# Column sums of modulation blocks in a diffusion-transformer step on one core: TensorE products with ones, or TensorE transposes summed by ScalarE

## The chip, the core and the metric

The kernel runs on one core of one Trainium2 chip. Its engines are TensorE (PE for its matmuls, PEld for its weight loads), VectorE (DVE), ScalarE (ACT), GpSimd (POOL) and SyncE (SP, which issues nearly all DMAs). Each engine works through its own instructions in the order in which they were written and waits on semaphores that the others raise. The metric is the device time of one execution in microseconds. The median of the runs is quoted.

## What is computed

One layer of an inference step for 1024 latent tokens and 256 context tokens, width 1024, in float32. What matters here is the modulation. From the conditioning vectors `c` (latent) and `c_ctx` (context) it makes six vectors of 1024 for each of the two token groups, and these shift, scale and gate the layer's two halves:

```python
def _modulation(cond, w_mod, b_mod):
    m = jax.nn.silu(cond) @ w_mod + b_mod
    return jnp.split(m[:, None, :], N_MOD, axis=-1)
...
    shift1, scale1, gate1, shift2, scale2, gate2 = mod
    h = _rmsnorm(x, norm1_g) * (1 + scale1) + shift1
    u = h @ w_in
    ...
    x = x + gate1 * (merged @ w_out)
    h2 = _rmsnorm(x, norm2_g) * (1 + scale2) + shift2
    a, b = jnp.split(h2 @ w_gu, 2, axis=-1)
    x = x + gate2 * ((jax.nn.silu(a) * b) @ w_down)
```

`u` feeds three mixers: neighbourhood attention, a pooling mixer and a convolution module. A final RMSNorm follows.

## The kernel before

**Number format of the matmuls.** A large product is done in three matmuls (`products`, L152): weights and activations are split into an upper part rounded to a shorter format and the rest (hi, lo, AH, AL). ACT makes the upper parts and DVE or POOL the lower ones.

**Three stages** follow each other: the front (`front_engines`: norm, input projection, pooling and convolution mixers; up to about 332 us), attention with the gate projections beside it (`attention_engines`), and the rear (`rear_engines`: output projections, second norm, and the FFN from about 1080 us on).

**The front.** The input projection has 18 units of 128 output channels, each in three token chunks `(u, c)` of 512, 512 and 256 columns. PE runs 24 matmuls a chunk and writes them to banks 0 to 3 of PSUM in a ring. A bank is given back by ACT, or, for units 1 and 3 and the channel mean, by DVE (`after`, `freed`). Banks 4 and 5 serve transposes of keys and values.

**Modulation.** The first two vectors (shift1, scale1) are made by PE at the start. The other four are made with little work for PE: DVE multiplies a block of `w_mod` by the conditioning values, one value for each row, and adds up eight such row groups (`modulation(n)` of the vector engine, L822 and L825), which leaves 128 partial sums in the partitions for each output channel. What is left to do is to sum over the partitions, so that the result has channels in the partitions. PE does this by a matmul with the accumulator as weights and a column of ones as the moving operand.
- *Late blocks* (gate1, shift2, scale2): n = 0 to 11, each of 256 channels for two token groups, thus four products of 128x128 with 128x1 (L441). Their results go to 48 columns of bank 7 (`modp`). `MOD_AT` (L115) says after which chunk PE does block n: n = 0 after (2, 2), 1 and 2 after (3, 0) and (3, 1), 3 and 4 after (4, 0) and (4, 1), 5 after (5, 0), 6 after (13, 2), 7 after (14, 0), 8 and 9 after (15, 0) and (15, 1), 10 after (16, 1), 11 after (17, 0). `mod_acc` has two buffers, so DVE waits in block n for PE's block n-2. At the end of the front ACT copies the 48 columns out at once (L805), and DVE adds the bias (`late_mod`).
- *The second gate* (gate2): n = 0 to 7, each of 128 channels, thus two products (L2411), with one accumulator `gate2_acc`. Their results go to 16 columns of bank 7 (`MOD_BANK`). ACT copies them out at p = 8 (L2825), and DVE adds the bias at p = 9 (`gate2_bias`).

**The FFN's order.** It goes over pairs p of hidden tiles with a seven-product scheme (P1 to P7, and X0, X1 for the context tokens). PE's order is `PRODUCTS`: for pair p it ends with P1 of pair p+1, then P4 and P3 of p, and right after P3 comes `gate2_products(p)`. The products go through a ring of banks 0 to 6. ACT's iteration p copies weights of pair p+1 to their upper parts (`upper_slot`, L2654, eight in all), copies P1 of p+1 (`copy_product`), and, when p is even, does the Silu of five quarters (`gate_quarter`, L2677). The last of them, "12", stands at the iteration's end and needs `add(p, "12")` of DVE (L3033), which needs P3 of p. POOL makes the lower parts of the slots (L2881), and DVE the weight sums in between.

**Other lines that are named:** L143 and L261 (`freed`, `after`), the evacuations L633 to L645 and L794 (the pool products), L833 (DVE's GLU product of unit 1 or 3, whose end frees banks), L452 (channel mean), L477 and L485 (transposes of keys and values), L1360 and L1367 on (attention on ACT).

Of the kernel before, what the change touches and what calls it, by code (L numbers as in the profile page):

```python
# [16 lines left out]
ACT = mybir.ActivationFunctionType  # L17
# [3 lines left out]
P = 128  # L21
D = 1024
KD = D // P
# [146 lines left out]
def front_engines(g, W, held):  # L170

    nc = g.nc
    with ExitStack() as ctx:
# [71 lines left out]
        STEPS = 2 * KD  # L245
        modp = g.aux[:, 1, 0:2 * 3 * KD]
        banks = g.ps_all[:, 0:2, :]
# [160 lines left out]
        def tensor(pe):  # L408
# [26 lines left out]
            def modulation(n):  # L435

                pe.wait_ge(acc_step, STEPS * (n + 1))
                for m in range(2):
                    for j in range(2):
                        c = 4 * n + 2 * m + j  # L440
                        mm = nc.tensor.matmul(modp[:, c:c + 1], mod_acc[:, n % 2, j, m * P:(m + 1) * P],  # L441
                                              g.ones[:, 0:1], start=True, stop=True)
                mm.then_inc(mod_used, 1)
# [171 lines left out]
        def scalar(act):  # L615
# [31 lines left out]
            def token_major(u, parts):  # L647
# [8 lines left out]
                for part in parts:  # L656
# [4 lines left out]
                    nc.scalar.activation(vt[:, a:b, :], flip[:, (at + part) % 2, 0:(b - a) * P].rearrange("p (t n) -> p t n", n=P), ACT.Copy).then_inc(tok_ready, 1)  # L661

            def cached_k_out():
                act.wait_ge(ck_turned, 1)
                for h in range(2):
                    nc.scalar.activation(cached_kT[:, 2 * h:2 * h + 2, :], flip[:, h, :].rearrange("p (a t) -> p a t", a=2), ACT.Copy).then_inc(ck_out, 1)
# [95 lines left out]
            for u in range(MIX):  # L762
# [6 lines left out]
                for c in range(3):  # L769
                    if u not in (0, 1, 3):  # L770
                        evacuate(u, c)
                    if c != 1 and U_V < u <= U_Q:
                        token_major(u - 1, (0, 1) if c == 0 else (2,))
                if u and u + 2 <= MIX and u != U_POOL:
                    split(u + 2)
# [21 lines left out]
                if u == 15:  # L797
                    for t in range(2):
                        act.wait_ge(ln_step, 1 + 2 * (t + 1))
                        for n, at in ((LAT, 0), (CTX, CCTX)):  # L800
                            x = conv[:, t, at:at + n]
                            nc.scalar.activation(x, x, ACT.Silu, bias=g.cols[:, OFF["cn_b"] + t:OFF["cn_b"] + t + 1],
                                                 scale=g.cols[:, OFF["cn_g"] + t:OFF["cn_g"] + t + 1]).then_inc(silu_ready, 1)
            act.wait_ge(mod_used, NG)
            nc.scalar.activation(g.mod[:, 2 * KD:5 * KD, :], modp.rearrange("p (m j) -> p m j", j=2), ACT.Copy).then_inc(mod_out, 1)  # L805

        def vector(dve):
# [78 lines left out]
            def late_mod():  # L886
                dve.wait_ge(mod_out, 1)
                mod = g.mod[:, 2 * KD:5 * KD, :]
                nc.vector.tensor_tensor(mod, mod, g.cols[:, OFF["b_mod"] + 2 * KD:OFF["b_mod"] + 5 * KD].rearrange("p (m j) -> p m j", j=1).broadcast_to([P, 3 * KD, 2]),
                                        ALU.add).then_inc(mod_step, 1)  # L890
                dve.wait_ge(mod_step, 1)
                mod_gain(g, 1, "norm2_g", 4, mod_step)
# [847 lines left out]
def rear_engines(g, G, sem, attention):  # L1740
# [3 lines left out]
    with ExitStack() as ctx:  # L1744
# [24 lines left out]
        gate2_acc = at("gate2_acc", [P, 2, P], N0 + 16384)  # L1769
        w_gate2 = W.raw[:, :].rearrange("p (k n) -> p k n", n=P)  # L1770
        hidden_in = at("hidden_in", [P, KD, T], -20480 - ROW)
        raw_rows = at("w_down_rows", [P, KD, T], -20480 - 2 * ROW)
# [523 lines left out]
        def tensor(pe):  # L2296
# [109 lines left out]
            def gate2_products(n):  # L2406
                if n == 0:
                    pe.wait_ge(*released(last_ring_job(MOD_BANK)))
                pe.wait_ge(acc_step, STEPS * (n + 1))
                for j in range(2):  # L2410
                    mm = nc.tensor.matmul(g.ps_all[:, MOD_BANK, 2 * n + j:2 * n + j + 1], gate2_acc[:, j, :], g.ones[:, 0:1], start=True, stop=True)  # L2411
                mm.then_inc(gate2_done, 1)

            def down_bank_wait(name, m):
                if name in ("P1", "P2"):
                    n = 4 * ROUND[name] + m
                    if n == MOD_BANK:
                        pe.wait_ge(gate2_out, 1)
                    else:
                        pe.wait_ge(*product_read(*[product for i, product in enumerate(RINGED) if i % PRODUCT_RING == n][-1]))  # L2420
                elif name != "ctx":
                    pe.wait_ge(*emptied(DOWN_PRODUCTS[ROUND[name] - 2], m))
                elif m % 2 == 0:
                    pe.wait_ge(*emptied("P5", m // 2))
# [116 lines left out]
        def scalar(act):  # L2541
# [114 lines left out]
            def copy_product(p):  # L2656
# [8 lines left out]
                nc.scalar.activation(temp[TEMP["11"][side]][:, :], g.ps_all[:, product_bank(p, "P1"), :], ACT.Copy).then_inc(copied, 1)  # L2665

            def gate_quarter(i, name):
                p = 2 * i
# [129 lines left out]
            for p in range(PAIRS_FFN):  # L2798
# [22 lines left out]
                if side == 0:  # L2821
                    gate_quarter(i, "12")
                if p == KD:
                    act.wait_ge(gate2_done, KD)
                    nc.scalar.activation(g.mod[:, 5 * KD:6 * KD, :], g.ps_all[:, MOD_BANK, 0:2 * KD].rearrange("p (m j) -> p m j", j=2), ACT.Copy).then_inc(gate2_out, 1)  # L2825
            for n in range(len(DOWN)):
# [84 lines left out]
        def vector(dve):  # L2911
# [149 lines left out]
            def gate2_bias():  # L3061
                dve.wait_ge(gate2_out, 1)
                gate2_mod = g.mod[:, 5 * KD:6 * KD, :]
# [414 lines left out]
```

## Time and profile before

| what | value |
|---|---|
| median of 3 runs | 1873.34 us (1871.3 to 1873.45) |
| profiled execution | 1871.09 us, span 1869.3 us |
| PE busy | 1847.3 us, 99% |
| DVE busy | 1145.8 us, 61% |
| ACT busy | 758.2 us, 41% |
| POOL busy | 543.7 us, 29% |
| granted clock of PE | 0.998 of full speed |

The span is the time from the first to the last record of the profiled execution. A timeline row gives the start, the length, the engine, the line, what it writes and reads, its form and how many like it were merged. The time in square brackets is how long the engine stood idle before it, with the instruction that released it. Ends of matmuls are modelled, and a matmul of 512 columns reads 0.39 us while the next begins 0.23 us after it. So the cost of something to PE is read from starts, not from lengths. A float32 product with ones shows as two matmul records, a transpose as one. Times of ACT and DVE are lengths of single instructions, which overlap a little at their ends.

### The profile page before, as it was taken

How to read it: one execution, taken by the hardware profiler on the slowest of the kernel's cores; microseconds unless marked ns; L12 is line 12 of the kernel's file. 1: busy time of each engine (PE TensorE's matmuls, PEld its weight loads, DVE VectorE, ACT ScalarE, POOL GpSimd, SP SyncE). 2: the span in 40 equal slices, each digit the busy share in tenths (PEclk: the TensorE clock that was granted, in tenths of full speed). 3: DMA queues.
4: the chain of work that ended last, by engine and by line, in shares of the span. 5: the costliest groups of instructions: out<-in, count | busy, mean ns of one | idle time of the engine just before them, and what ended most of it. 6: DMA issues, size and time to landing. Idle time of an engine off the chain costs nothing.

```text
span 1869.3 us, 27109 instructions
## 1 busy us (share of the span) xinstructions
PE 1847.3 (99%) x10106; PEld 1587.0 (85%) x10106; DVE 1145.8 (61%) x2142; ACT 758.2 (41%) x1444; POOL 543.7 (29%) x407
## 2 busy tenths in 40 slices
PE   8999999999999999999999999999999999999998
PEld 3788888888888888888888888888888888888898
DVE  4799996156566655366317855554434434789984
ACT  5612232355555564454313522222222222545464
POOL 0000000455555552144532144444344441000000
PEclk9999999999999999999999999999999999999999
DMA  8472545464444532756532222221222224866665
GB/s 325 161 221 62 148 128 192 120 151 115 112 119 112 126 95 75 239 169 185 180 116 68 82 77 96 96 84 58 74 74 74 74 74 150 283 209 224 210 212 204
DMA packets 243466, 260.52 MB, mean 139 GB/s; under 512 B 50696, under 2 KB 182280, under 8 KB 242312
## 3 DMA queue, kind: packets, MB, share of 16 engines
q1 hardware_dynamic: 243336, 258.80, 44.8%
q8 instruction: 81, 1.33, 0.3%
q14 instruction: 49, 0.40, 0.1%
HBM read 196.09 MB, written 62.65 MB: 138 GB/s over the span
## 4 chain that ended last, share of the span: by engine, by line
PE 90%; DVE 4%; DMA 2%; ACT 2%; issue 1%; POOL 0%; SPq 0%; ACTq 0%; DVEq 0%; POOLq 0%
PE ps_all L152 68%; PE ps_all L2452 5%; PE ps_all L2454 4%; PE ps_all L2453 4%; PE ps_all L1315 2%; PE ps_all L1301 2%; DVE mod_acc L825 1%; PE ps_all L1287 1%; DMA wmod_then_mixers<-w_mod_dram 1%; PE ps_all L1292 1%; PE ps_all L537 1%; DMA wmod_block<-w_mod_dram 1%; DVE Y L3114 0%; POOL KB L1520 0%; PE ps_all L2486 0%
## 5 line engine op out<-in xcount | busy, mean ns | idle before, releaser
L152 PE MATMUL ps_all<-AH,w_hi 128*128 128x512 f32 (+1 forms) x1376 | 493.7, 359 | 2.4 <-ACT gate_rows L1360 1.3
L152 PE MATMUL ps_all<-AH,w_lo 128*128 128x512 f32 (+1 forms) x1376 | 483.1, 351 | 0.0
L152 PE MATMUL ps_all<-AL,w_hi 128*128 128x512 f32 (+1 forms) x1376 | 483.0, 351 | 0.0
L152 PEld LDWEIGHTS ps_all<-AH,w_lo 128*128 128x128 f32 x1376 | 259.9, 189 | 36.0
L152 PEld LDWEIGHTS ps_all<-AH,w_hi 128*128 128x128 f32 x1376 | 260.2, 189 | 34.3 <-DVE AL L909 2.0
L152 PEld LDWEIGHTS ps_all<-AL,w_hi 128*128 128x128 f32 x1376 | 260.5, 189 | 30.1
L3033 DVE TENSOR_TENSOR quarter<-ps_all,quarter 128x512 f32<-128x512 f32 x140 | 96.6, 690 | 176.6 <-PE ps_all L152 174.6
L2881 POOL TENSOR_TENSOR slot_lo<-w_pair,slot_hi 128x512 fp32r<-128x512 f32 x96 | 129.9, 1378 | 174.0 <-ACT slot_hi L2654 174.0
L152 PE MATMUL ps_all<-AH,slot_hi 128*128 128x256 f32 (+1 forms) x384 | 129.5, 337 | 0.0
L152 PE MATMUL ps_all<-AL,slot_hi 128*128 128x256 f32 (+1 forms) x384 | 129.2, 336 | 0.0
L152 PE MATMUL ps_all<-AH,slot_lo 128*128 128x256 f32 (+1 forms) x384 | 129.1, 336 | 0.0
L2881 POOL TENSOR_TENSOR w_lo<-w_pair,w_hi 128x512 fp32r<-128x512 f32 x64 | 85.4, 1356 | 114.4 <-ACT w_hi L2654 114.4
L1469 DVE TENSOR_TENSOR PT<-ps_all,PT 128x384 fp32r<-128x384 f32 (+1 forms) x144 | 63.7, 479 | 79.7 <-ACT PT L1378 79.6
L1538 POOL TENSOR_SCALAR prob<-prob,softmax_cols 128x640 f32<-128x640 f32 (+1 forms) x80 | 60.5, 756 | 130.5 <-DVE softmax_cols L1462 125.4
L1367 ACT ACTIVATE prob<-ps_all,softmax_cols 128x256 f32<-128x256 f32 x80 | 38.0, 474 | 137.4 <-DVE softmax_cols L1452 123.9
L845 DVE SCALAR_TENSOR_TENSOR xT_then_mixers<-wmod_then_mixers,cols,xT_then_mixers 128x1295 f32<-128x1295 f32 x60 | 89.4, 1573 | 0.0
L2452 PE MATMUL ps_all<-AH 128*128 128x512 f32 (+1 forms) x248 | 86.9, 350 | 1.1 <-DVE AL L3069 1.1
L1514 POOL TENSOR_TENSOR w_lo<-w_raw,w_hi 128x1024 fp32r<-128x1024 f32 x21 | 50.5, 2404 | 124.6 <-ACT w_hi L1338 124.6
L2454 PE MATMUL ps_all<-AH,AL 128*128 128x512 f32 (+1 forms) x248 | 86.3, 348 | 0.0
L2453 PE MATMUL ps_all<-AL,AH 128*128 128x512 f32 (+1 forms) x248 | 86.3, 348 | 0.0
L2452 PE MATMUL ps_all<-AH,w_hi 128*128 128x512 f32 (+1 forms) x236 | 83.9, 355 | 0.0
L2454 PE MATMUL ps_all<-AH,w_lo 128*128 128x512 f32 (+1 forms) x236 | 83.3, 353 | 0.0
(309 smaller groups left out, 4084.6 us busy)
## 6 DMA issues: line engine op xcount, KB each, us to landing
w_raw<-w_in_dram SPq DMA_DIRECT2D x42, 512.0 KB
w_pair<-w_gu_dram SPq DMA_DIRECT2D x20, 1024.0 KB, 5.3
hidden_in<-hidden SPq DMA_DIRECT2D x77, 256.0 KB, 3.5
wmod_then_mixers<-w_mod_dram SPq DMA_DIRECT2D x19, 1024.0 KB, 8.0
hidden<-quarter SPq DMA_DIRECT2D x50, 256.0 KB, 2.1
branch_and_gates<-gates SPq DMA_DIRECT2D x16, 768.0 KB, 4.4
w_down_rows<-w_down_dram SPq DMA_DIRECT2D x44, 256.0 KB, 3.7
gates<-gate_rows SPq DMA_DIRECT2D x42, 256.0 KB, 2.5
```

What stands on the lines that cost most here:

```text
L152: mm = nc.tensor.matmul(out, w, a[:, k, cols[0]:cols[1]], start=(first and part == 0), stop=(last and part == 2))
L845: nc.vector.scalar_tensor_tensor(conv[:, t, :], glu[:, t, k:k + CV], w, conv[:, t, :], ALU.mult, ALU.add).then_inc(conv_step, 1)
L1301: mm = nc.tensor.transpose(psT[:, turned_at(j):turned_at(j) + P], prob[:, s % 3, j * P:(j + 1) * P], g.ident[:, :])
L1367: nc.scalar.activation(pr[:, LOCAL:PCOLS], psS_past, ACT.Exp, bias=c[:, 2:3], accum_out=c[:, 4:5]).then_inc(past_ready, 1)
L1469: nc.vector.tensor_tensor(PT[:, s % 2, j0:j1, P:2 * P], psT[:, turned_at(j0):turned_at(j0) + (j1 - j0) * P].rearrange("p (j n) -> p j n", ...
L1514: nc.gpsimd.tensor_tensor(W.lo[:, u % 2, :], W.raw[:, :], W.hi[:, u % 2, :].bitcast(F32), ALU.subtract).then_inc(W.lo_ready, 1)
L1538: nc.gpsimd.tensor_scalar(pr[:, a:PCOLS], pr[:, a:PCOLS], c[:, 5:6], 1.0, ALU.mult, ALU.mult).then_inc(normal, 1)
L2452: nc.tensor.matmul(out, wh, th, start=first, stop=False)
L2453: nc.tensor.matmul(out, wh, tl, start=False, stop=False)
L2454: return nc.tensor.matmul(out, wl, th, start=False, stop=last)
L2881: nc.gpsimd.tensor_tensor(tiles4(lo), in_pair(p, idx), tiles4(hi.bitcast(F32)), ALU.subtract).then_inc(s_lo, 1)
L3033: nc.vector.tensor_tensor(temp[TEMP[out][side]][:, :], g.ps_all[:, product_bank(p, source), :], temp[TEMP[first][side]][:, :], ALU.add).th ...
```

## The change

PE no longer multiplies the accumulator blocks by ones. It turns each 128x128 block by a transpose, which puts channels in partitions and the partial sums along the free axis. ACT then copies each turned block onto itself in PSUM, and its accumulator output, the sum along the free axis, goes straight to the block's column of `g.mod`.

In the front the turned blocks of n go to the whole of bank 6 or bank 7 in turn. PE waits before block n for ACT's sums of block n-2, and ACT does `mod_sums(n)`, four copies, right after the chunk's evacuation and the token-major copies. The copy of 48 columns is gone, and DVE's `late_mod` waits for all 12 sums.

For the second gate both turned blocks of n go to the same 256 columns of bank 7 each time. PE waits in group n for ACT's sums of group n-1, and ACT does `gate2_sums(p-1)`, two copies, at the end of its iteration p, for p = 1 to 8. The copy of 16 columns is gone.

```diff
@@ -243,7 +243,7 @@
         STEPS = 2 * KD
-        modp = g.aux[:, 1, 0:2 * 3 * KD]
+        mod_turns = g.aux
         banks = g.ps_all[:, 0:2, :]
@@ -435,11 +435,12 @@
                 pe.wait_ge(acc_step, STEPS * (n + 1))
+                if n >= 2:
+                    pe.wait_ge(mod_out, n - 1)
                 for m in range(2):
                     for j in range(2):
-                        c = 4 * n + 2 * m + j
-                        mm = nc.tensor.matmul(modp[:, c:c + 1], mod_acc[:, n % 2, j, m * P:(m + 1) * P],
-                                              g.ones[:, 0:1], start=True, stop=True)
+                        at = (2 * m + j) * P
+                        mm = nc.tensor.transpose(mod_turns[:, n % 2, at:at + P], mod_acc[:, n % 2, j, m * P:(m + 1) * P], g.ident[:, :])
                 mm.then_inc(mod_used, 1)
@@ -660,6 +661,15 @@
+            def mod_sums(n):
+                act.wait_ge(mod_used, n + 1)
+                for m in range(2):
+                    for j in range(2):
+                        at, row = (2 * m + j) * P, 2 * KD + 2 * n + m
+                        last = nc.scalar.activation(mod_turns[:, n % 2, at:at + P], mod_turns[:, n % 2, at:at + P], ACT.Copy,
+                                                    accum_out=g.mod[:, row, j:j + 1])
+                last.then_inc(mod_out, 1)
+
             def cached_k_out():
@@ -771,6 +781,8 @@
                         token_major(u - 1, (0, 1) if c == 0 else (2,))
+                    for n in MOD_AT.get((u, c), ()):
+                        mod_sums(n)
                 if u and u + 2 <= MIX and u != U_POOL:
@@ -801,8 +813,6 @@
                                                  scale=g.cols[:, OFF["cn_g"] + t:OFF["cn_g"] + t + 1]).then_inc(silu_ready, 1)
-            act.wait_ge(mod_used, NG)
-            nc.scalar.activation(g.mod[:, 2 * KD:5 * KD, :], modp.rearrange("p (m j) -> p m j", j=2), ACT.Copy).then_inc(mod_out, 1)
@@ -884,7 +894,7 @@
             def late_mod():
-                dve.wait_ge(mod_out, 1)
+                dve.wait_ge(mod_out, len(MOD_AT))
                 mod = g.mod[:, 2 * KD:5 * KD, :]
@@ -1768,6 +1778,7 @@
         w_gate2 = W.raw[:, :].rearrange("p (k n) -> p k n", n=P)
+        gate2_turned = lambda j: g.ps_all[:, MOD_BANK, j * P:(j + 1) * P]
         hidden_in = at("hidden_in", [P, KD, T], -20480 - ROW)
@@ -2407,15 +2418,17 @@
                 pe.wait_ge(acc_step, STEPS * (n + 1))
+                if n:
+                    pe.wait_ge(gate2_out, n)
                 for j in range(2):
-                    mm = nc.tensor.matmul(g.ps_all[:, MOD_BANK, 2 * n + j:2 * n + j + 1], gate2_acc[:, j, :], g.ones[:, 0:1], start=True, stop=True)
+                    mm = nc.tensor.transpose(gate2_turned(j), gate2_acc[:, j, :], g.ident[:, :])
                 mm.then_inc(gate2_done, 1)
             def down_bank_wait(name, m):
                 if name in ("P1", "P2"):
                     n = 4 * ROUND[name] + m
                     if n == MOD_BANK:
-                        pe.wait_ge(gate2_out, 1)
+                        pe.wait_ge(gate2_out, KD)
                     else:
@@ -2663,6 +2676,12 @@
                 nc.scalar.activation(temp[TEMP["11"][side]][:, :], g.ps_all[:, product_bank(p, "P1"), :], ACT.Copy).then_inc(copied, 1)
+
+            def gate2_sums(n):
+                act.wait_ge(gate2_done, n + 1)
+                for j in range(2):
+                    last = nc.scalar.activation(gate2_turned(j), gate2_turned(j), ACT.Copy, accum_out=g.mod[:, 5 * KD + n, j:j + 1])
+                last.then_inc(gate2_out, 1)
@@ -2820,9 +2839,8 @@
                     gate_quarter(i, "12")
-                if p == KD:
-                    act.wait_ge(gate2_done, KD)
-                    nc.scalar.activation(g.mod[:, 5 * KD:6 * KD, :], g.ps_all[:, MOD_BANK, 0:2 * KD].rearrange("p (m j) -> p m j", j=2), ACT.Copy).then_inc(gate2_out, 1)
+                if 1 <= p <= KD:
+                    gate2_sums(p - 1)
             for n in range(len(DOWN)):
@@ -3059,7 +3077,7 @@
             def gate2_bias():
-                dve.wait_ge(gate2_out, 1)
+                dve.wait_ge(gate2_out, KD)
                 gate2_mod = g.mod[:, 5 * KD:6 * KD, :]
```

## Rows read from the trace of the kernel before

**Rows 1.** The page: PE's busy time, and the chain that ended last, by engine.

```profile
PE 1847.3 (99%) x10106; PEld 1587.0 (85%) x10106; DVE 1145.8 (61%) x2142; ACT 758.2 (41%) x1444; POOL 543.7 (29%) x407
...
PE 90%; DVE 4%; DMA 2%; ACT 2%; issue 1%; POOL 0%; SPq 0%; ACTq 0%; DVEq 0%; POOLq 0%
```

**Rows 2.** PE's timeline around late block 5 (start us, us, what).

```profile
136.46 0.39 PE L152 MATMUL ps_all<-AH,w_lo 128*128 128x512 f32 x1
136.69 0.95 PE L441 MATMUL ps_all<-ones,mod_acc 128*128 128x1 f32 x8
...
137.82 0.40 PE L152 MATMUL ps_all<-AL,w_hi 128*128 128x512 f32 x1
```

**Rows 3.** The same around eight transposes of value tiles.

```profile
164.97 0.39 PE L152 MATMUL ps_all<-AH,w_lo 128*128 128x512 f32 x1
165.20 1.03 PE L485 MATMUL ps_all<-ident,xT_then_mixers 128*128 128x128 f32 x8
...
166.31 0.40 PE L152 MATMUL ps_all<-AL,w_hi 128*128 128x512 f32 x1
```

**Rows 4.** The same around two transposes of key tiles.

```profile
224.57 0.39 PE L152 MATMUL ps_all<-AH,w_lo 128*128 128x512 f32 x1
224.80 0.38 PE L477 MATMUL ps_all<-ident,xT_then_mixers 128*128 128x128 f32 x2
...
225.25 0.39 PE L152 MATMUL ps_all<-AL,w_hi 128*128 128x512 f32 x1
```

**Rows 5.** The same around group 2 of the second gate.

```profile
1152.48 0.39 PE L152 MATMUL ps_all<-AH,slot_lo 128*128 128x512 f32 x1
1152.71 0.50 PE L2411 MATMUL ps_all<-ones,gate_acc 128*128 128x1 f32 x4
...
1153.39 0.40 PE L152 MATMUL ps_all<-AL,slot_hi 128*128 128x512 f32 x1
```

**Rows 6.** DVE's and PE's timelines before PE's wait near 122 us.

```profile
101.77 0.62 DVE L822 TENSOR_SCALAR mod_acc<-wmod_then_mixers,silu_c 128x256 f32<-128x256 f32 x2 [3.76 <-DMA wmod_then_mixers<-w_mod_dram]
...
121.87 0.50 PE L152 MATMUL ps_all<-AH,w_hi 128*128 128x512 f32 x1 [0.16 <-DVE wmod_then_mixers L833]
```

**Rows 7.** Timelines of late block 10: DVE's sums, PE's last matmul before.

```profile
305.39 5.63 DVE L825 SCALAR_TENSOR_TENSOR mod_acc<-wmod_then_mixers,silu_c,mod_acc 128x256 f32<-128x256 f32 x14
...
312.43 0.39 PE L152 MATMUL ps_all<-AH,w_lo 128*128 128x512 f32 x1
```

**Rows 8.** ACT's timeline at the front's end: copies of 256 and of 48 columns.

```profile
331.36 0.39 ACT L645 ACTIVATE xT_then_mixers<-ps_all 128x256 f32<-128x256 f32 x1 [2.27 <-PE ps_all L152]
331.64 0.20 ACT L805 ACTIVATE mod<-ps_all 128x48 f32<-128x48 f32 x1
```

**Rows 9.** ACT's timeline in attention: the accumulator's read and what follows it.

```profile
601.67 0.19 ACT L1367 ACTIVATION_READ_ACCUMULATOR prob<-ps_all,softmax_cols 128x1 f32 x1
601.76 0.60 ACT L1369 ACTIVATE prob<-prob,softmax_cols 128x384 f32<-128x384 f32 x1
```

**Rows 10.** ACT's timeline: the first evacuation of the pool products.

```profile
267.94 0.69 ACT L794 ACTIVATE wmod_then_mixers<-ps_all,cols 128x512 f32<-128x512 f32 x1 [1.61 <-PE ps_all L463]
```

**Rows 11.** DVE's and ACT's timelines around group 2 of the second gate.

```profile
1152.98 0.69 DVE L3033 TENSOR_TENSOR quarter<-ps_all,quarter 128x512 f32<-128x512 f32 x1 [1.27 <-PE ps_all L152]
...
1153.84 0.61 ACT L2677 ACTIVATE quarter<-quarter 128x512 f32<-128x512 f32 x1
1154.36 1.14 ACT L2654 ACTIVATE slot_hi<-w_pair 128x512 fp32r<-128x512 f32 x2
```

**Rows 12.** ACT's and PE's timelines before group 1 of the second gate.

```profile
1124.90 2.20 ACT L2654 ACTIVATE slot_hi<-w_pair 128x512 fp32r<-128x512 f32 x4 [1.66 <-PE ps_all L152]
...
1127.13 0.39 PE L152 MATMUL ps_all<-AH,slot_lo 128*128 128x512 f32 x1
```

**Rows 13.** Windows: busy time of PE, PEld, DVE, ACT, POOL, then PEclk, DMA share, GB/s.

```profile
50.00:55.00 5.00, 4.78 (x13) 2.99 (x14) 3.85 (x7) 4.94 (x9) 0.00 (x0) 0.74 1.08 358
...
122.00:232.00 110.00, 110.00 (x590) 94.42 (x591) 108.31 (x90) 24.42 (x42) 0.00 (x0) 1.00 0.42 114
```

## The prediction

> **What bounds the kernel now.** I read the page first, then the chain, then the timelines around the places that the change touches. PE is busy for 99% of the span and carries 90% of the chain that ended last [rows 1]. So a microsecond taken from PE's own queue is worth a microsecond wherever PE isn't waiting for another engine, and a new wait in that queue costs its full length. The late modulation products and the second gate's products stand in PE's queue between matmuls that run without a gap. Both savings and waits are read there.
>
> **What a block costs PE.** I measure from the start of the last matmul before a group to the start of the second matmul after it, since the first one after is irregular. Around a late block, which is four products with ones in eight passes, that is 137.82 - 136.46 = 1.36 us [rows 2]. Around eight transposes of the same 128x128 f32 form it is 166.31 - 164.97 = 1.34 us [rows 3], around two 225.25 - 224.57 = 0.68 us [rows 4]. One transpose is thus worth (1.34 - 0.68) / 6 = 0.11 us, and four would give 0.90 us: a late block saves 0.46 us. A group of the second gate, two products in four passes, takes 1153.39 - 1152.48 = 0.91 us [rows 5], and two transposes 0.68 us: it saves 0.23 us.
>
> **Late blocks 0 to 3: nothing.** At 121.87 PE waits 0.16 us for the GLU product of DVE, which frees a bank. DVE comes to it late because it sat idle for 3.76 us at 101.77 until a block of w_mod had landed [rows 6], and then worked without a break. Nothing in that stretch depends on when PE finishes its blocks, so 4 x 0.46 us saved before this place only lengthens PE's wait there.
>
> **Late blocks 4 to 11: 8 x 0.46 = 3.68 us, less one clip.** DVE's chain is tied to PE again by the channel mean near 232 us, after which PE saves on blocks 6 to 9 and DVE doesn't, 4 x 0.46 = 1.84 us in all. Block 10 is added up by 305.39 + 5.63 = 311.02, and PE could load it at 312.43 [rows 7]: a margin of 1.41 us, so 0.43 us of the gain turns into a wait. I count 3.25 us gained.
>
> **ACT's new work in the front.** The trace has no ACTIVATE of 128 columns and none that writes PSUM. A copy of 256 columns takes 0.39 us and the next begins 0.28 us after it, one of 48 columns takes 0.20 us [rows 8]; between them, 128 columns give 0.28 us, and the next can start after 0.17 us. The accumulator read behind it takes 0.19 us and lets the next instruction start after 0.09 us [rows 9]. Four sums take 4 x 0.26 + 0.10 = 1.14 us. ACT's queue is in order, so each block holds back what follows. The shortest gap is after block 6: the evacuation of the pool products begins at 267.94 after 1.61 us idle [rows 10]. The sums fit. PE's new wait there, for the sums of two blocks earlier, is met in every block: even the nearest, block 2 for block 0, comes two chunks later. Cost nothing, covered by ACT's idle time; without it the pool evacuation would be late, and two more banks stand between that and PE. DVE's late bias no longer waits for a copy at the end, which nobody needed then. Should each pair cost as the 256-column row plus a full read, 0.39 + 0.19 = 0.58 us, four are 2.3 us and pass the 1.61 us by 0.7 us, still inside those banks.
>
> **The second gate: the place that decides.** With one region of bank 7 used again, PE must wait in group n until ACT has summed group n-1. ACT does those sums at the end of its iteration p = n, while PE asks for them right after P3 of the same pair. No row shows this wait, so I build it.
> - Group 0 has no such wait: -0.23 us.
> - Groups 2, 4 and 6: ACT's iteration is even and ends with the Silu of quarter "12". That needs DVE's addition of P3's bank, which begins at 1152.98 and lasts 0.69 us, and ACT starts the Silu at 1153.84; its next instruction begins at 1154.36 [rows 11]. Only there can the sums start. Two sums take 0.17 + 0.09 + 0.17 + 0.19 = 0.62 us, to 1154.98; 0.05 us for the signal is my estimate. PE, which loaded these weights from 1152.48 on, now begins at 1155.03. From a load with nothing before it to the second matmul after the group I take 0.60 us (the 0.68 less the wait behind a running matmul): 1155.63 in place of 1153.39 [rows 5], +2.24 us with the saving included. The two later places have the same shape, so 3 x 2.24 = +6.72 us. Queued behind PE's waiting transposes are all matmuls of the next pair, and nothing gives the time back, as PE waits nowhere else until the end.
> - Groups 1, 3, 5 and 7: the iteration is odd and has no Silu. ACT's three slot copies (0.52 us apart, the first at 1124.90) are done at 1126.46; the sums end at 1127.08, and PE wants them at 1127.13 [rows 12]. With the signal that is level: 0 to 0.1 us, I take 0.05 us. 4 x (0.05 - 0.23) = -0.72 us.
> - The sums also push ACT's next two slot copies by about 0.52 us. POOL is still at work on the slots before them on even pairs, and on odd pairs the second copy waits for PE anyway: nothing.
>
> **Sum:** -3.25 - 0.23 + 6.72 - 0.72 = +2.5 us. The profiled execution took 1871.09 us (span 1869.3 and 1.8 around it), so 1873.6 us like for like. It stands 2.25 us under the median of the runs, 1873.34 us. I add the 2.5 us to the median: 1875.9 us, 0.13% up. About 0.2%, 3.75 us, is what a measurement of this kernel can tell from no change.
>
> **Bounds of the unknown price.** If two sums cost nothing, the even groups lose 0.62 us less each and the odd ones save in full: +0.5 us. If they cost 2 x 0.58 = 1.16 us, the even ones lose 0.54 us more each, the odd ones 0.5 us more each: +2.5 + 1.6 + 2.1 = +6.2 us. I take 0.62 us, because two rows on either side in columns bracket it. The Trainium skill, "ScalarE: Activation LUTs" (What ACT_TABLE_LOAD costs), gives an ACTIVATE with immediate scale and bias as 186 ns + 0.833 ns a column and 93 ns of overlap. By that estimate two sums would take 0.68 us and the result be +2.9 us; no row here shows the 128-column form.
>
> **Rivals.**
> 1. *The waits don't arise* and only the savings count. It would need ACT to have the sums of n-1 before the Silu, or DVE to add P3's bank without waiting for P3. The order of ACT's instructions in the code speaks against it, and so does the Silu at 1153.84, over 1 us after P3's last matmul. It gives -3.25 - 8 x 0.23 = -5.1 us: 1868.2 us, faster. Chance 0.08.
> 2. *Dear sums.* ACT reads and writes the bank in place, and the pair costs more than the interpolation says. Then the level race of the odd groups is lost as well, and seven groups pay. From 0.80 us for two sums on the result passes +3.75 us; at 1.16 us it is +6.2 us: 1879.5 us, slower. For it speaks that no row shows the form, against it that the rows for copy and read are regular. Chance 0.19.
> 3. *The front's gain is not carried* through attention, where PE's order and the DMAs of ACT's and DVE's inputs interlock. Then +2.5 + 3.25 = +5.8 us: 1879.1 us. Against it: the chain from 340 us on starts from PE's own matmuls, and attention's first loads wait for a store of PE's last unit. Chance 0.07.
> 4. *The clock falls* in the three waits of some 2.3 us. Around 50 us PE was busy in pieces only, and the granted clock was 0.74 over 5 us [rows 13], half of the time at 1.2 GHz; such a fall costs some 1.3 us. Three give +2.5 + 3.9 = +6.4 us: 1879.7 us. Against it: PE has no gap in the 20 us before each wait. The Trainium skill, "TensorE: Matmul & The Clock Gate" (Part 4: PE-mode transpose), says that transposes don't count as activity for the clock as matmuls do. The stretch from 122 to 232 us, in which the eight of [rows 3] stand with others like them, had a granted clock of 1.00 [rows 13], so the trace doesn't bear it out for bursts of this size. Chance 0.03.
> 5. *A transpose is no cheaper than the ones products* it replaces. Then the savings vanish and the even waits stay at some 2.5 us: +7.7 us, 1881.0 us. The rows of two forms in this trace speak against it. Chance 0.03.
>
> **How the numbers follow.** The forecast has 0.60 and nearly all of it lies within 0.2%. Slower is rivals 2 to 5, 0.32 less the part of 2 and 3 that stays under 3.75 us, so 0.31 with a little of the forecast's upper end. Faster is rival 1 with a bit: 0.09. Same is 0.60. The range takes in the forecast's bounds, +0.5 to +6.2 us, widened below by the scatter of the runs (2 us): 1871.8 to 1879.5 us.
>
> **What the profile would show.** Right: line 441's and 2411's matmuls gone, 48 and 16 transposes in their place; PE waiting on ACT before the gate transposes, some 2.2 us in three places and next to nothing in four; the sums at 0.28 us with reads of 0.19 us; PE's wait near 121.8 us longer by 1.8 us; attention starting about 3.2 us earlier. Wrong: no wait of PE on ACT around 1155 us, or waits in all seven; sums longer than 0.4 us; a granted clock below 1.00 between 1080 and 1310 us; attention starting at its old time.

## The result, and the profile after

The changed kernel takes 1880.09 us (median of 6 runs, 1877.72 to 1882.89) beside 1873.38 us (6 runs, 1871.30 to 1874.72) for the kernel before: a ratio of 1.0039 with a 95% interval of 1.0029 to 1.0049. That is slower by 6.7 us, where +2.5 us were forecast, and 0.6 us above the range. The profiled execution took 1880.99 us with a span of 1879.2 us.

The page first: PE's busy time, and the chain that ended last, which stand against [rows 1].

```profile
PE 1846.5 (98%) x10042; PEld 1581.8 (84%) x10042; DVE 1146.5 (61%) x2142; ACT 776.6 (41%) x1570; POOL 542.9 (29%) x407
...
PE 87%; DVE 6%; DMA 2%; ACT 2%; issue 2%; POOL 1%; SPq 0%; ACTq 0%; DVEq 0%; POOLq 0%
```

PE has 64 matmuls fewer (128 passes over a column of ones went, 64 transposes came) and is busy for 0.8 us less, yet the span grew by 9.9 us. Most of this profile's loss thus lies between PE's instructions. Not all of it does: at the rows' prices the transposes save 12 x 0.46 + 8 x 0.23 = 7.4 us of busy time, and only 0.8 us of that is seen. The table of PE's waits after the change says behind whom PE was idle (us in total, times, longest):

```profile
PE ps_all L2424 <- ACT ps_all L2683: 6.9, 3, 2.3
PE ps_all L1311 <- POOL prob L1548: 2.2, 2, 2.0
...
PE ps_all L443 <- DVE mod_acc L835: 1.6, 1, 1.6
PE ps_all L152 <- DVE wmod_then_mixers L843: 1.5, 1, 1.5
```

The first line is the wait that the change adds: the second gate's transposes (line 2424) behind ACT's sums (line 2683), three times 2.3 us and in no other group. The last two lines are the places in the front that the prediction named, block 10 and the GLU product.

**The savings are what the rows of before promised.** PE's timeline around late block 5 and around group 1 of the second gate, after the change:

```profile
135.65 0.39 PE L152 MATMUL ps_all<-AH,w_lo 128*128 128x512 f32 x1
135.88 0.60 PE L443 MATMUL ps_all<-ident,mod_acc 128*128 128x128 f32 x4
...
136.55 0.39 PE L152 MATMUL ps_all<-AL,w_hi 128*128 128x512 f32 x1
...
1128.16 0.39 PE L152 MATMUL ps_all<-AH,slot_lo 128*128 128x512 f32 x1
1128.39 0.38 PE L2424 MATMUL ps_all<-ident,gate_acc 128*128 128x128 f32 x2
...
1128.84 0.40 PE L152 MATMUL ps_all<-AL,w_hi 128*128 128x512 f32 x1
```

From the matmul before a group to the second one after it, the block takes 136.55 - 135.65 = 0.90 us, as interpolated, in place of 1.36 us [rows 2]. The odd group takes 1128.84 - 1128.16 = 0.68 us with no wait in front of it, so the level race of the odd groups is won.

**The even groups wait as built.** ACT's and then PE's timeline around group 2:

```profile
1154.63 0.61 ACT L2696 ACTIVATE quarter<-quarter 128x512 f32<-128x512 f32 x1
1155.15 0.26 ACT L2683 ACTIVATE ps_all<-ps_all 128x128 f32<-128x128 f32 x1
1155.35 0.18 ACT L2683 ACTIVATION_READ_ACCUMULATOR ps_all<-ps_all 128x1 f32 x1
1155.43 0.26 ACT L2683 ACTIVATE ps_all<-ps_all 128x128 f32<-128x128 f32 x1
1155.63 0.18 ACT L2683 ACTIVATION_READ_ACCUMULATOR ps_all<-ps_all 128x1 f32 x1
...
1155.95 0.41 PE L2424 MATMUL ps_all<-ident,gate_acc 128*128 128x128 f32 x2 [2.29 <-ACT ps_all L2683]
```

Silu, two sums one after the other, then PE. The sums take 1155.15 to 1155.81, 0.66 us, where 0.62 us was assumed. (The Trainium skill, "ScalarE: Activation LUTs", What ACT_TABLE_LOAD costs, gives 186 ns + 0.833 ns a column for an ACTIVATE with immediate scale and bias, by which 128 columns would take an estimated 0.29 us; the row says 0.26 us.)

**What the sum didn't hold: the clock.** Windows at and right behind the waits. The columns are the window, the busy time of PE, PEld, DVE, ACT and POOL with their counts, then PE's granted clock, the DMA share and GB/s:

```profile
1153.00:1157.00 4.00, 1.71 (x9) 1.15 (x9) 0.69 (x1) 3.85 (x11) 3.24 (x3) 1.00 0.00 0
1157.00:1161.00 4.00, 4.00 (x12) 3.10 (x11) 0.00 (x0) 0.00 (x0) 2.98 (x3) 0.57 0.58 176
1209.00:1213.00 4.00, 2.73 (x13) 2.35 (x14) 0.00 (x0) 2.17 (x8) 4.00 (x4) 1.00 0.05 3
1263.00:1267.00 4.00, 4.00 (x12) 3.25 (x13) 0.00 (x0) 0.82 (x2) 3.95 (x4) 0.58 0.32 87
384.00:388.00 4.00, 3.41 (x13) 2.87 (x14) 1.18 (x3) 2.50 (x7) 4.00 (x5) 0.71 0.73 172
```

From 1157 to 1161 us PE is busy without a break, but gets 12 matmuls done where it does some 17 at full speed (one each 0.23 us): most of that window runs at the lower level, 1.2 GHz. The same stands behind the wait of group 6 at 1263 us, and not behind that of group 4 (1209 to 1213 us, and the 4 us after it have 1.00 too). The last row is a fall in attention, where PE had waited 2.01 us for POOL at 384.59.

To see where the time went I compared the starts of the same matmuls in both profiles, along the span. The difference (after less before) is:

| place in the span of before | difference, us | what lies between |
|---|---|---|
| 80 us | 0.0 | |
| 181 us | -1.28 | blocks 0 to 5, less PE's wait near 121.5 us, 1.53 in place of 0.16 us |
| 302 us | -3.12 | blocks 6 to 9 |
| 323 us | -2.19 | block 10: a wait of 1.62 us; block 11 |
| 403 us | +1.31 | POOL wait and clock fall at 384 to 389 us |
| 1070 us | +1.28 | attention and the work up to the feed-forward part |
| 1311 us | +9.94 | the second gate |
| 1548 us | +9.94 | nothing is given back |

Across the second gate the difference grows by 8.66 us. Three even groups, one first and four odd groups make 5.4 us of it by their rows, near the 5.77 us of the forecast; two clock falls of some 1.6 us each are the rest. The 1.6 us is read at a fall itself: within a few us behind group 2 the difference goes from 3.04 to 4.65 us, with no wait in between.

### The profile page after: what moved, and what is told of

It is laid out like the page before. It is cut to its first block, busy times and chain, and to the rows that moved or that the text cites. A ratio compares the mean times of both kernels' runs of the same rounds, so it can differ in the third digit from the quotient of the medians.

```text
span 1879.2 us, 27124 instructions
## 1 busy us (share of the span) xinstructions
PE 1846.5 (98%) x10042; PEld 1581.8 (84%) x10042; DVE 1146.5 (61%) x2142; ACT 776.6 (41%) x1570; POOL 542.9 (29%) x407
## 3 DMA queue, kind: packets, MB, share of 16 engines
q8 instruction: 80, 1.31, 0.3%
## 4 chain that ended last, share of the span: by engine, by line
PE 87%; DVE 6%; DMA 2%; ACT 2%; issue 2%; POOL 1%; SPq 0%; ACTq 0%; DVEq 0%; POOLq 0%
PE ps_all L152 65%; PE ps_all L2465 4%; PE ps_all L2466 4%; PE ps_all L2467 4%; PE ps_all L1325 2%; PE ps_all L1311 2%; DVE mod_acc L835 1%; PE ps_all L1297 1%; PE ps_all L1302 1%; DMA wmod_then_mixers<-w_mod_dram 1%; PE ps_all L538 1%; DMA wmod_block<-w_mod_dram 1%; DVE Y L3132 0%; DVE sig L890 0%; PE ps_all L2499 0%
```

## The experiments

The question was whether the missing time belongs to the waits, and by which way: to the transposes or to the waiting. Each kernel ran in five rounds beside the kernel before.

**1. The two halves apart.** The first kernel takes the front as changed and leaves the second gate as before; the second the other way round. The diff of the first against the changed kernel, at its core:

```diff
-                if n:
-                    pe.wait_ge(gate2_out, n)
                 for j in range(2):
-                    mm = nc.tensor.transpose(gate2_turned(j), gate2_acc[:, j, :], g.ident[:, :])
+                    mm = nc.tensor.matmul(g.ps_all[:, MOD_BANK, 2 * n + j:2 * n + j + 1], gate2_acc[:, j, :], g.ones[:, 0:1], start=True, stop=True)
```

> Only the front is changed, the second gate is as before. Theory 'absorbed': PE reaches 350 us about 2.2 us earlier than before, but the loads and POOL's work at the start of attention don't come earlier by as much, so by 400 us its lead is 0 to 0.5 us, and the time is 0 to 0.5 us below before, or 1 to 2 us above it where the granted clock falls near 385 us. Rival 'carried': what was lost near 385 us in the profile of the change was an accident of that execution; the lead of 2.2 us is still there at 400 us and the time is 2.2 us below before (ratio 0.9988).

> Only the second gate is changed, the front is as before. Theory 'waits and clock': three waits of PE on ACT of 2.3 us, which is +5.5 us (3 x 2.24 - 0.25 - 4 x 0.24), and in some of the executions a fall of the granted clock after a wait, each +1.6 us: +5.5 to +10 us, mean near +8. Rival 'waits alone': +5.5 us in every execution, granted clock 1.00 from 1080 to 1310 us.

The front alone took 1870.49 us (11 runs) beside 1872.49 (21 runs): 0.9986, interval 0.9977 to 0.9995, a gain. The second gate alone took 1881.83 us (5 runs) beside 1871.88 (15 runs): 1.0049, interval 1.0035 to 1.0063. Its waits are the same as in the full change, and so is the granted clock over the whole stretch. The wait row, and the window over the second gate:

```profile
PE ps_all L2414 <- ACT ps_all L2673: 6.9, 3, 2.3
...
1080.00:1310.00 230.00, 223.13 (x1178) 191.87 (x1177) 117.52 (x245) 61.20 (x131) 96.16 (x72) 0.99 0.25 82
```

So the whole loss is the second gate's. The difference of starts grows by 8.66 us in this stretch here too, with two falls behind three waits (groups 4 and 6 here, 2 and 6 in the full change). In the front kernel the difference is -2.69 us at 323 us, -0.50 of it from before the change's first place, so -2.19 us, the same as in the profile of the full change. It is -2.89 us at 403 us and the same afterwards until a clock fall at 979 us. The front's gain is therefore carried through attention, and the loss near 384 us belongs to the one execution that was profiled.

**2. ACT's sums near the start of its iteration p instead of its end.** The same edit in the kernel with the second gate alone and in the full change:

```diff
                     upper_slot(n)
                     upper_slot(n + 1)
+                if 1 <= p <= KD:
+                    gate2_sums(p - 1)
                 if side == 0:
                     gate_quarter(i, "11")
 ...
                     gate_quarter(i, "12")
-                if 1 <= p <= KD:
-                    gate2_sums(p - 1)
```

> The front as before, the second gate changed, but ACT does the sums of group n-1 right after the first two slot copies of its iteration n, ahead of all Silus. Theory 'waits and clock': 1.9 us below before (ratio 0.9990), no wait of PE on ACT, clock 1.00 from 1080 to 1310 us. Rival: the transposes themselves, not the wait, make the clock fall; then there are still falls between 1080 and 1310 us, and the time is at or above before.

> Both parts changed, ACT's sums for the second gate early as in the run of the second gate alone, which stood 1.9 us below before. Theory 'absorbed': the front's part is worth 0 to 0.5 us or costs 1 to 2 us where the clock falls near 385 us, so the time is 1.5 us below to 0.5 us above before. Rival 'carried': 4.1 us below before (ratio 0.9978). PE doesn't wait for ACT's second-gate sums in either.

With the second gate alone: 1869.99 us (11 runs) beside 1871.88, 0.9989, interval 0.9980 to 0.9997. With both: 1868.50 us (11 runs) beside 1872.49, 0.9983, interval 0.9974 to 0.9992. No wait of PE on ACT is left in the gate; the row of its window in the first of the two reads

```profile
1080.00:1310.00 230.00, 230.00 (x1229) 198.91 (x1228) 119.91 (x248) 66.34 (x143) 102.75 (x78) 1.00 0.26 82
```

PE is busy all 230 us at full clock, and the difference of starts falls by 2.08 us in this stretch, near the 8 x 0.23 = 1.84 us that rival 1 of the prediction counted. Both medians are what the theory of waits and a carried front expected (1.9 and 4.1 us below; measured 1.9 and 4.0). Against experiment 1's second kernel, the place of the sums alone is worth 11.8 us of median (1881.83 - 1869.99, the same chip).

**3. The wait without the transposes.** The ones products stay, and only PE's wait for ACT is put in, behind one-column copies that follow Silu "12":

```diff
+                if n:
+                    pe.wait_ge(gate2_out, n)
                 for j in range(2):
                     mm = nc.tensor.matmul(g.ps_all[:, MOD_BANK, 2 * n + j:2 * n + j + 1], gate2_acc[:, j, :], g.ones[:, 0:1], start=True, stop=True)
 ...
+                if 1 <= p <= KD:
+                    act.wait_ge(gate2_done, p)
+                    for j in range(2):
+                        last = nc.scalar.activation(g.mod[:, 5 * KD + p - 1, j:j + 1], g.ps_all[:, MOD_BANK, 2 * p - 2 + j:2 * p - 1 + j], ACT.Copy)
+                    last.then_inc(gate2_out, 1)
```

> The kernel before with its ones products in both places, and only the wait added: in iteration n of ACT, behind the Silu of quarter 12, the two columns of group n-1 are copied out, and PE waits for that in group n. The wait of groups 2, 4, 6 should be 2.29 - 0.56 + 0.2 = about 1.9 us. Theory 'the wait makes the clock fall': 3 x 1.9 = +5.7 us, and a fall of the granted clock after some of the three waits, +1.6 us each: +6 to +10 us. Rival 'the transposes make it fall': +5.7 us and a clock of 1.00 from 1080 to 1310 us.

It took 1883.83 us (5 runs) beside 1872.07 (21 runs): 1.0061, interval 1.0047 to 1.0074, the slowest of all. That is +11.8 us, above the +6 to +10 us that were expected. One of its waits, and the windows behind the three of them:

```profile
1157.08 0.58 PE L2413 MATMUL ps_all<-ones,gate_acc 128*128 128x1 f32 x4 [1.84 <-ACT mod L2828]
...
1158.00:1162.00 4.00, 4.00 (x12) 3.09 (x12) 0.00 (x0) 0.00 (x0) 3.54 (x3) 0.57 0.41 122
1213.00:1217.00 4.00, 4.00 (x13) 3.19 (x12) 0.00 (x0) 0.00 (x0) 2.91 (x3) 0.60 0.54 180
1267.00:1271.00 4.00, 4.00 (x12) 3.13 (x11) 0.00 (x0) 0.00 (x0) 3.25 (x3) 0.57 0.51 163
```

The wait is shorter than the changed kernel's (1.84 against 2.29 us), and the clock falls behind all three. The difference of starts grows by 11.0 us across the gate, 3.67 us a wait: 1.84 us of waiting, about 0.2 us to start again, and 1.6 us of the fall. So transposes aren't needed for a fall. The Trainium skill, "TensorE: Matmul & The Clock Gate" (Part 4: PE-mode transpose), says that transposes don't count as activity in the same way. This run doesn't single them out: here the products with one column did no better in the same place, with 3 falls behind 3 waits against 4 behind 6.

**4. Shorter waits.** The second gate alone, with the sums between the slot copies 6 and 7, and right before Silu "12":

```diff
                     for idx in range(5, 8):
                         upper_slot(n + idx)
+                        if idx == 6 and 1 <= p <= KD:
+                            gate2_sums(p - 1)
```

```diff
+                if 1 <= p <= KD:
+                    gate2_sums(p - 1)
                 if side == 0:
                     gate_quarter(i, "12")
```

> Second gate alone changed, ACT's sums between the slot copies 6 and 7 of its iteration, 1.04 us earlier than in the change: waits of 2.29 - 1.04 = 1.25 us in groups 2, 4 and 6. Waits alone: 3 x (2.24 - 1.04) - 0.25 - 4 x 0.24 = +2.4 us. Theory 'the clock falls by the length of the wait': fewer falls than in the change, +2.4 to +4 us. Rival 'any wait does it': +2.4 + 3.2 = +5.6 us or more.

> Second gate alone changed, ACT's sums right before the Silu of quarter 12, 0.52 us earlier than in the change: waits of 1.77 us. Waits alone: 3 x (2.24 - 0.52) - 1.2 = +4.0 us. Theory: between the run with waits of 1.25 us and the one with 2.29 us also in the falls, +4 to +7 us.

After slot copy 6: 1875.11 us (11 runs) beside 1872.07, 1.0012, interval 1.0004 to 1.0021. Before Silu "12": 1876.74 us (11 runs), 1.0025, interval 1.0016 to 1.0034. The two kernels' wait rows, first the one and then the other:

```profile
PE ps_all L2414 <- ACT ps_all L2673: 3.8, 3, 1.3
```

```profile
PE ps_all L2414 <- ACT ps_all L2673: 5.3, 3, 1.8
...
1080.00:1310.00 230.00, 224.69 (x1199) 193.50 (x1198) 119.43 (x247) 64.47 (x137) 98.08 (x74) 1.00 0.25 81
```

Waits of 1.3 and of 1.8 us brought no fall in either profile: the clock of the whole gate is 1.00. The difference of starts grows by 2.3 and by 3.9 us, which is the waits and some 0.2 us each to start again, less the savings. The medians are up by 3.0 and 4.7 us, some 0.8 us more than that. The loss goes with the length of the wait, and the part by which it runs ahead of it comes with the longest ones.

| wait in an even group | operation behind it | kernels | from the last 512-column matmul before to the first after | falls behind the waits |
|---|---|---|---|---|
| 2.29 us | two transposes | full change, second gate alone | 2.84 us | 4 of 6 |
| 1.84 us | four passes over ones | wait alone | 2.66 us | 3 of 3 |
| 1.77 us | two transposes | sums before Silu "12" | 2.32 us | 0 of 3 |
| 1.25 us | two transposes | sums after slot copy 6 | 1.80 us | 0 of 3 |

The fourth column is the time between the starts of the two matmuls, the wait and the small operations together. Where a fall began inside it, it is longer than the number given.

These counts come from one execution of each kernel, and the one with the sums before Silu "12" was among the fastest of its 11. But every run has its mean granted clock on record, and one less that clock, times the span, is the time lost to it. Each clock is rounded to 0.001, which is 1.9 us, so only averages say something. Averaged over the runs of a kernel and taken above that of the kernel before beside it, it is 4.5 us for the second gate alone (5 runs), 5.9 us for the wait alone (5 runs), 0.5 us for the sums before Silu "12" and 0.6 us for the sums after slot copy 6 (11 runs each). So falls are rare in the last two in all their runs, and could be much of their 0.8 us. It also means that the second and third rows, whose waits differ by 0.07 us, don't differ by chance. What makes the difference, the operation behind the wait or the longer time without a 512-column matmul (2.66 against 2.32 us), no run here tells apart.

**5. Block 10's load.** In the changed kernel, as before it, SP issues block 10's w_mod load behind the weights of unit 17. This kernel is experiment 2's full version with that load moved ahead of them:

```diff
+                if u == 15:
+                    load_mod(10)
                 if 0 < u <= MIX - 2:
                     load_w(u + 2)
 ...
-                    load_mod(n)
+                    if n != 10:
+                        load_mod(n)
                     load_mod(n + 1)
```

> Both parts changed with early sums for the second gate, and the load of late block 10 issued by SP before the weight load of unit 17 instead of behind it. Theory 'block 10 waits for its load': DVE's 8.8 us idle before block 10 shrinks, PE's wait of 1.1 to 1.6 us before it is gone, and the whole is 1.1 to 1.6 us faster than both parts with early sums (which stood about 3.2 us below before): 4.3 to 4.8 us below before, ratio 0.9976. Rival: attention's start gives that back, 3.2 us below before.

It took 1865.87 us (5 runs) beside 1872.07: 0.9967, interval 0.9955 to 0.9980. SP's and DVE's timelines of this kernel, and PE's at block 10:

```profile
289.49 0.38 SPq L302 DMA_DIRECT2D wmod_then_mixers<-w_mod_dram  x1
...
296.58 0.62 DVE L835 TENSOR_SCALAR mod_acc<-wmod_then_mixers,silu_c 128x256 f32<-128x256 f32 x2
...
309.97 0.60 PE L446 MATMUL ps_all<-ident,mod_acc 128*128 128x128 f32 x4
```

DVE now begins at 296.58 in place of 305.11 us, and PE doesn't wait. From 80 to 323 us the difference of starts falls by 3.85 us, where it fell by 2.19 us in the changed kernel: the 1.6 us of block 10's wait come back. In its profile the clock stays at 1.00 through the gate. The median is 6.2 us down where 4.3 to 4.8 us were expected.

The load alone, moved in the kernel before:

> The kernel before, with only the load of late block 10 moved ahead of the weight load of unit 17. With ones products PE didn't wait for block 10, so theory: no change, ratio 0.9990 to 1.0010, and the earlier load's worth in the run with all three edits is what it gives back to the transposes. Rival: the earlier load is worth 2 us or more on its own, by what it does to the loads behind it; then the time is 2 us or more below before.

1872.85 us (11 runs) beside 1871.67 (18 runs): 1.0004, interval 0.9995 to 1.0013. By itself the move is worth nothing, since there PE came to block 10 later than DVE.

Last, the three edits together once more:

> The kernel with all three edits again, beside the one before it: 4.3 to 6.2 us below before (0.9967 to 0.9977). A clean repeat if the first ratio, 0.9967, lies in the new interval.

1866.42 us (8 runs) beside 1871.67: 0.9971, interval 0.9961 to 0.9981. It repeats the gain: 5.3 us here and 6.2 us above. Of the versions that beat the kernel before, this is the fastest: transposes and sums, ACT's sums ahead of the gate quarters, and block 10's load ahead of unit 17's weights.

## Why the prediction was wrong

**What held.** The savings of 0.46 us a block and 0.23 us a group are read off the rows after the change as 0.46 and 0.23. The first four blocks gave mostly a longer wait near 121.5 us, 1.53 us in place of 0.16 us, 1.4 us longer where 1.8 was forecast; "nothing" was not quite right, as PE went on at 121.51 us in place of 121.87 us. The sums cost 0.66 us with 0.62 forecast, so rival 2 (dear sums) didn't come about. PE waits on ACT in groups 2, 4 and 6, by 2.29 us, and not in the odd groups. An even group costs 2.24 us, to the digit what was forecast, with some luck: the sums took 0.04 us more, the 0.05 us for the signal was an estimate that no row bore, and the rows show 0.14 us from the end of the sums at 1155.81 to PE's start at 1155.95, while PE's way from there to the second matmul took 0.48 us in place of 0.60 us. The gate's own sum, +5.77 us, stands against 5.4 us in the rows. Rivals 1 and 5 fell with the same rows, and rival 3 with experiment 1: the front's gain is carried whole.

**Rival 4 decided, and had a chance of 0.03.** Its mechanism was named in the prediction with the right places and nearly the right price: 1.3 us each, where the runs show 1.6. The first step that failed is "Against it: PE has no gap in the 20 us before each wait", on which the sum put the clock at nothing. A busy stretch before the wait doesn't keep the clock: a wait of 2.29 us in PE's otherwise gapless queue was followed by a fall in 4 of 6 places. The rows of [rows 13] showed a fall where PE was busy in pieces; they said nothing on a single wait, since the kernel before has none in the stretch from 122 to 232 us. A wait with no counterpart in the trace needed a bound in the sum, up to 3 x 1.6 us, and not a rival of 3%. Had it been there, the range would have reached well past 1880.1 us.

**Block 10 was mis-sized.** That is the second step. The term "0.43 us of the gain turns into a wait" came to 1.62 us. DVE's sums and PE around block 10 after the change, with SP's issue of the load first; the row of before that stands against it is in [rows 7]:

```profile
296.74 1.85 SPq L302 DMA_DIRECT2D wmod_then_mixers<-w_mod_dram  x2
...
305.11 0.62 DVE L832 TENSOR_SCALAR mod_acc<-wmod_then_mixers,silu_c 128x256 f32<-128x256 f32 x2 [8.83 <-DMA wmod_then_mixers<-w_mod_dram]
305.64 5.63 DVE L835 SCALAR_TENSOR_TENSOR mod_acc<-wmod_then_mixers,silu_c,mod_acc 128x256 f32<-128x256 f32 x14
...
311.32 0.66 PE L443 MATMUL ps_all<-ident,mod_acc 128*128 128x128 f32 x4 [1.62 <-DVE mod_acc L835]
```

and the issue of the same load in the kernel before:

```profile
297.91 1.84 SPq L302 DMA_DIRECT2D wmod_then_mixers<-w_mod_dram  x2
```

The load was issued 1.17 us earlier than before, landed 0.25 us later, and DVE's chain ended at 311.27 us in place of 311.02. PE came to block 10 ahead by 3.12 us (the table), of which 1.28 us were there before blocks 6 to 9 (0.36 us past the wait near 121.5 us and two blocks of 0.46 us). The prediction counted only the 1.84 us of those four blocks against the margin of 1.41 us, on the ground that DVE's chain moves with PE up to the channel mean near 232 us and so has the rest as well. The issue of the load did move, by 1.17 us, but its landing didn't. So the full 3.12 us stood against the margin: 3.12 - 1.41 = 1.7 us, and 1.62 us were measured. The front gave 2.19 us instead of 3.25; the load moved in experiment 5 gives 3.85.

**The account of the 6.7 us.** The front -2.2 us and the gate's waits less savings +5.4 us make +3.2 us, 0.7 us over the forecast's +2.5. The remaining 3.5 us are the clock. The mean granted clock of the changed kernel's runs is 0.996, that of the kernel before about 0.998; experiment 2's full version, which has the same instructions and no waits in the gate, is back at 0.9975 over its runs, beside 0.9979 of the kernel before there. A difference of 0.002 over 1880 us is some 3.8 us. That these 3.5 us are about two falls of 1.6 us in a run is worked out, since only one execution of each kernel has the trace. By differences of starts it comes to nearly the same: -2.2 us of the front and +8.7 us across the gate make +6.5 us. The profiled executions are 9.9 us apart since the changed kernel's has PE's wait for POOL and the fall near 385 us on top (3.5 us).

## What to carry to other kernels

When an edit puts a wait of about two microseconds into a queue that is busy for 99% of the time, cost it as the wait plus a possible fall of the clock behind it (here 1.6 us on top of 2.3), even if the engine was busy without a break until then. Reusing one buffer for a chain of two engines is free only if the second engine's step stands early in its in-order queue: here the place of two 0.3 us sums was worth 11.8 us, more than all that the change itself could bring. And where savings pile up on one engine, look for the next transfer that doesn't move with it: its load must be issued earlier for the gain to pass.

## What the runs showed of the hardware

**A fall behind products of one column, without a wait.** At 979.90 us in the kernel before, and within 4 us of that in all others, PE takes sums over channels as products with a column of ones, 24 passes in 2.6 us, and never waits:

```profile
979.90 0.28 PE L2340 MATMUL ps_all<-ones,sumsq 128*128 128x1 f32 x2
...
982.49 0.49 PE L152 MATMUL ps_all<-AH,w_out_hi 128*128 128x512 f32 x1
```

In 8 of the 12 profiles a fall of the granted clock began at their last passes or up to 1.6 us behind them, between 979 and 985 us. There is none in those of the kernel before, the full change, the sums before Silu "12" and experiment 5's first kernel. From the last 512-column matmul before to the first after it is 2.8 us. A shorter stretch of the same kind near 1023 us, 16 passes and 1.9 us, had no fall in any of the 12. The windows of the kernel before and of experiment 2's kernel with the second gate alone:

```profile
980.00:985.00 5.00, 5.00 (x36) 4.55 (x35) 0.78 (x2) 2.18 (x3) 1.29 (x1) 1.00 0.00 0
```

```profile
980.00:985.00 5.00, 5.00 (x29) 4.37 (x29) 0.84 (x4) 2.18 (x3) 1.27 (x1) 0.79 0.00 0
```

PE is busy for all of the 5 us in both, with 36 matmuls in the one and 29 in the other (part of that is that the narrow products begin 0.5 us earlier in the second, and so more of them lie before the window). "Busy" by the profile is thus no guarantee of the clock, and such a fall is drawn anew in each execution: before's profile has none here, the profile of before with only one load moved has one. It costs the same 1.6 us. The scatter of 3 to 5 us among runs of one kernel goes with the clock: of 75 runs of the kernel before, the 24 with a mean granted clock of 0.999 took 1871.0 us on average, the 39 with 0.998 took 1872.5 us, and the 10 with 0.997 took 1873.4 us. That each such step is one of these falls is argued, since those runs have no trace.

**The load that was issued earlier and landed later** (296.74 to 305.11 us against 297.91 to 304.86 us) was not studied further; issued at 289.49 us it was there before DVE wanted it.
